# Sums of squares in a decoder trunk: VectorE joins pairs of squared channels into sums of four, TensorE adds two of them in place of four

## The reference, cut to what matters

```python
def rmsnorm(x, g):
    xf = x.astype(jnp.float32)
    y = xf * lax.rsqrt(jnp.mean(xf * xf, axis=-1, keepdims=True) + EPS)
    return (y * g.astype(jnp.float32)).astype(x.dtype)
...
        x = x + rmsnorm(mix, p['norm_mix_post'][l])
        h = rmsnorm(x, p['norm_ffn_pre'][l])
        f, buf = conv_ffn(h, conv_s0[l], p['ffn_w_gate'][l], p['ffn_w_up'][l], p['ffn_conv_w'][l],
                          p['ffn_conv_b'][l], p['ffn_w_down'][l])
        conv_bufs.append(buf)
        x = x + rmsnorm(f, p['norm_ffn_post'][l])
```

## Time and profile before

| what | us |
|---|---|
| median of 3 runs | 1463.52 |
| lowest and highest run | 1462.89, 1463.57 |
| span of the profiled execution | 1460.7 |
| the profiled execution's own time | not given apart from its span |
| TensorE busy | 1424.8 |
| VectorE busy | 910.8 |
| ScalarE busy | 676.9 |
| GpSimd busy | 562.9 |

### The profile page before, as it was taken

How to read it: one execution, slowest core, us unless ns; L and a number is a source line. 1 busy time by engine, 2 the same in 40 slices (tenths; PEclk the granted TensorE clock), 3 DMA queues, 4 the chain that set the end, 5 groups by cost and what they waited for, 6 DMA issues and landing times.

```text
span 1460.7 us, 31008 instructions
## 1 busy us (share of the span) xinstructions
PE 1424.8 (98%) x11156; PEld 1300.5 (89%) x11156; DVE 910.8 (62%) x1506; ACT 676.9 (46%) x1281; POOL 562.9 (39%) x552
## 2 busy tenths in 40 slices
PE   7999999999999999999999999999999999999997
PEld 6999999999999999998986666766989999999997
DVE  5732437599999992226457643443579999995323
ACT  5333345366666672216313544543275666665111
POOL 2342111145555553431330044441325655553433
PEclk9999999999999999999999999999999999999998
DMA  4243322222222333222321099981313222222231
GB/s 167 74 144 99 119 73 102 92 87 88 95 106 89 112 109 100 79 94 83 113 73 33 15 285 289 282 262 40 116 34 116 88 95 106 89 95 99 80 102 64
DMA packets 56714, 160.19 MB, mean 110 GB/s; under 512 B 7633, under 2 KB 27602, under 8 KB 55330
## 3 DMA queue, kind: packets, MB, share of 16 engines
q1 hardware_dynamic: 50466, 137.82, 28.3%
q0 software_dynamic: 6144, 20.98, 4.7%
HBM read 150.72 MB, written 8.05 MB: 109 GB/s over the span
## 4 chain that ended last, share of the span: by engine, by line
PE 45%; DVE 5%; issue 2%; ACT 1%; POOL 0%; SPq 0%; DMA 0%; POOLq 0%; ACTq 0%; DVEq 0%
PE lin L2287 15%; PE lin L2641 12%; PE lin L2859 4%; PE px L2898 2%; PE px L2936 2%; PE lin L2357 1%; PE px L2903 1%; PE px L2867 1%; PE px L2847 1%; PE lin L2813 1%; PE lin L2793 1%; PE px L2414 1%; PE px L2922 0%; PE lin L2830 0%; PE lin L2829 0%
## 5 line engine op out<-in xcount | busy, mean ns | idle before, releaser
L717 POOL TENSOR_TENSOR w_l<-w_raw,w_h 128x1408 fp32r<-128x1408 f32 (+1 forms) x50 | 143.9, 2878 | 271.6 <-ACT w_h L838 150.1
L712 POOL TENSOR_TENSOR w_l<-w_raw,w_h 128x1024 fp32r<-128x1024 f32 (+2 forms) x42 | 108.2, 2575 | 276.7 <-ACT w_h L838 266.9
L2287 PE MATMUL lin<-xg_h,w_h 128*128 128x272 f32 x848 | 194.1, 301 | 13.2 <-DVE xg_l L1458 10.6
L2287 PE MATMUL lin<-xg_l,w_h 128*128 128x272 f32 x848 | 183.5, 288 | 0.0
L2287 PE MATMUL lin<-xg_h,w_l 128*128 128x272 f32 x848 | 183.4, 288 | 0.0
L2641 PE MATMUL lin<-xq_h,w_h 128*128 128x272 f32 x576 | 166.4, 289 | 3.8 <-DVE xq_l L1844 2.2
L2641 PE MATMUL lin<-xq_h,wq_r 128*128 128x272 f32 x864 | 169.3, 289 | 0.6 <-ACT part L1133 0.6
L2641 PE MATMUL lin<-xq_h,w_l 128*128 128x272 f32 x576 | 166.0, 288 | 0.0
L2641 PE MATMUL lin<-xq_l,w_h 128*128 128x272 f32 x576 | 165.4, 287 | 0.0
L2287 PEld LDWEIGHTS lin<-xg_h,w_h 128*128 128x128 f32 x848 | 136.9, 189 | 20.8 <-issue 13.8
L838 ACT ACTIVATE w_h<-w_raw 128x1024 fp32r<-128x1024 f32 (+2 forms) x71 | 77.3, 1089 | 167.1 <-PE lin L2287 140.0
(11 more groups left out here) (407 smaller groups left out, 3231.4 us busy)
## 6 DMA issues: line engine op xcount, KB each, us to landing
wq_raw<-w SPq DMA_DIRECT2D x38, 1024.0 KB, 4.9
w_raw<-w SPq DMA_DIRECT2D x61, 512.0 KB, 3.5
w_raw<-w SPq DMA_DIRECT2D x30, 704.0 KB, 4.1
pages<-cache SPq DMA_DIRECT2D x128, 160.0 KB, 3.8
pages<-cache POOLq DMA_DIRECT2D x128, 160.0 KB, 3.9
St<-state SPq DMA_DIRECT2D x4, 1024.0 KB, 5.6
gla_s<-St SPq DMA_DIRECT2D x4, 1024.0 KB, 3.9
w_raw<-w SPq DMA_DIRECT2D x4, 576.0 KB, 3.6
```

Of the source, the lines that this page charges most:

```text
L712: g.tensor_tensor(w_l[:, p % 2, 0:n], raw_panel(p)[:, 0:n], w_h[:, p % 2, 0:n].bitcast(F32), ALU.subtract).then_inc(w_lo, 1)
L717: g.tensor_tensor(w_l[:, p % 2, 0:n], w_raw[:, p % 2, 0:n], w_h[:, p % 2, 0:n].bitcast(F32), ALU.subtract).then_inc(w_lo, 1)
L2287: last = mm(lin[:, 2 * out_set + half, 0:HALF], w[:, slot, (w0 + k) * P:(w0 + k + 1) * P], (v[ch] if isinstance(v, list) else v[:, ch, :]) ...
```

## The change

The second pair sum of each two is followed by one more addition on VectorE, which joins the two pair sums in `pair_sum[1]` (the tile `rstd_x`) and counts a new semaphore, `quad_sum`. TensorE sums `pair_sum[1]` twice per statistic, after channel 4 and ahead of channel 7, in place of four pair sums. `sums_before` counts two in place of four for the three statistics, and ScalarE's `rstd` waits for two. VectorE's wait on `stat_ps` asks for nothing beyond the earlier statistics at the first three pairs, and for the first of the two sums at the fourth (`m // 3`).

```diff
--- before.py
+++ after.py
@@ -305,6 +305,7 @@
         gla_in = sem("gla_in")
         xh_done, xl_done = sem("xh_done"), sem("xl_done")
         sq_done, sq_used = sem("sq_done"), sem("sq_used")
+        quad_sum = sem("quad_sum")
         stat_ps, stat_ln, rstd_done = sem("stat_ps"), sem("stat_ln"), sem("rstd_done")
         t_done, x_done, xv_done = sem("t_done"), sem("x_done"), sem("xv_done")
         y_out = sem("y_out")
@@ -488,7 +489,7 @@
 
         def sums_before(n):
 
-            return sum(4 if k in BY_PAIR else 1 for k in range(n))
+            return sum(2 if k in BY_PAIR else 1 for k in range(n))
 
         def first_halves(n):
 
@@ -865,7 +866,7 @@
             def rstd(n, width, out, too=None):
 
                 if n in BY_PAIR:
-                    act.wait_ge(stat_ps, sums_before(n) + 4)
+                    act.wait_ge(stat_ps, sums_before(n) + 2)
                 else:
                     act.wait_ge(sq_used, SQ_BASE[n] + SQ_LEN[n])
                 fn(out[:], px[:, 0:2, 0:HALF], ACT.Ln, scale=1.0 / width, bias=col("eps")).then_inc(stat_ln, 1)
@@ -1720,8 +1721,11 @@
                     if ch % 2:
                         i, m = i0 + ch, ch // 2
                         dve.wait_ge(sq_done, i + 1)
-                        dve.wait_ge(stat_ps, sums_before(n + 1) + max(m - 1, 0))
+                        dve.wait_ge(stat_ps, sums_before(n + 1) + m // 3)
                         v.tensor_tensor(pair_sum[m % 2], sq[:, (i - 1) % 2, :], sq[:, i % 2, :], ALU.add).then_inc(sq_used, 2)
+                        if m % 2:
+                            dve.wait_ge(sq_used, i + 1)
+                            v.tensor_tensor(pair_sum[1], pair_sum[0], pair_sum[1], ALU.add).then_inc(quad_sum, 1)
 
             def ffn(layer, pa, ta, pb, tb_, n_stat):
                 f0, us0, ps_, ts_ = layer * FC, layer * US_ALL, pa + 2 * PLAIN, ta + 2 * PLAIN
@@ -2376,15 +2380,14 @@
                 for k in range(DC):
                     pe.wait_ge(xh_done, before + k + 1)
                     if k == DC - 1:
-                        pair_squares(n + 1, k - 2)
-                        pair_squares(n + 1, k)
+                        quad_squares(n + 1, 1)
                     for m in range(DIRECT - 1 if n == 3 and k == DC - 2 else DIRECT):
                         for j in range(k - 1, k + 1) if n == 3 and m and k == DC - 1 else (k,):
                             last = direct_chunk(t + m, w[:, m, :], x_, j, (1,) if j < AHEAD[n] else (0, 1))
                         if k == DC - 1:
                             last.then_inc(tile_done, 1)
-                    if k in (2, 4):
-                        pair_squares(n + 1, k - 1)
+                    if k == 4:
+                        quad_squares(n + 1, 0)
 
             def first_panels(p, t, arrive, n):
 
@@ -2414,12 +2417,12 @@
                     last = mm(px[:, half, 0:HALF], ones[:], src[:, half * HALF:(half + 1) * HALF], start=start, stop=stop)
                 return last
 
-            def pair_squares(n, k):
-
-                if k == 1:
+            def quad_squares(n, k):
+
+                if k == 0:
                     pe.wait_ge(stat_ln, n)
-                pe.wait_ge(sq_used, SQ_BASE[n] + k + 1)
-                ones_matmuls(pair_sum[k // 2 % 2], k == 1, k == SQ_LEN[n] - 1).then_inc(stat_ps, 1)
+                pe.wait_ge(quad_sum, 2 * BY_PAIR.index(n) + k + 1)
+                ones_matmuls(pair_sum[1], k == 0, k == 1).then_inc(stat_ps, 1)
 
             def stat_sum(n):
```

## The result

The changed kernel takes 1477.62 us (median of 4 runs, 1476.68 to 1478.05) against 1463.2 for the kernel before (4 runs, 1462.26 to 1463.57): +14.4 us, ratio 1.010, 95% interval 1.0087 to 1.0114. It lies 2.0 us above the top of the range. The forecast way was right, the size was not. The spans differ by 15.7 (1476.4 against 1460.7), 1.3 more than the medians. The slowest of the four runs, 1478.05, is the profiled one, and 1.65 us lie outside its span. That and the 0.4 by which 1478.05 lies above its own median make the 1.3.

The account below looks back on a forecast made before the run. The prediction took a VectorE and ScalarE chain from pair 2's sum to bound each site's end, not TensorE. Lateness of 3.59 + 1.53 + 3.59 = +8.7 us on 1463.52 gave 1472.2 us, range 1467.6 to 1475.6.

Parts of the forecast that it names:

- What bounds the sites: Events 0, 1, 2 (sites A, B, C): a VectorE and ScalarE chain sets the end; TensorE's removed work is worth 0.
- The tie at A: Event 0, 284 to 304 us: TensorE starts its fourth pair sum at 300.69, VectorE's fourth pair sum ends at 300.63.
- the wait at B: Event 1, 668 to 688 us: TensorE's fourth pair sum starts at 684.02 after idling for VectorE's, begun at 683.25.
- the chain from pair 2: At each site's end: pair 2's sum, squares of channels 6 and 7, pair 3's sum; lateness passes one for one.
- removed sums: Two of four TensorE sums go per site, 0.96 us each, 1.92 together; forecast worth 0.
- First join, +0.77: VectorE's join of pairs 0 and 1, ahead of channel 6's residual: all later VectorE work comes 0.77 us later.
- what it pushes into: Events 0 and 2: channel 7's addition meets GpSimd's w_l, which goes first; pair 2's sum ends at 300.78 at event 0.
- Second join, on the path whole: VectorE's join of pairs 2 and 3, ahead of TensorE's last sum: wholly on the path, 303.50 to 304.22 at event 0.
- The chain's sum, +8.7: Lateness of TensorE's last sum at events 0, 1 and 2: 3.59 + 1.53 + 3.59 = +8.7 us.
- TensorE's clock, not in the sum: 4.5 us idle gaps at events 0 and 2: nothing to about 1.45 us each; nothing taken, 2.9 for both as upper end.
- Rival 3: TensorE's clock falls in one or both long gaps, events 0 and 2: +10.2 to +11.6, 1473.7 to 1475.1 us; chance 18%.
- Nothing taken up behind the sites: Stages behind the sites give nothing back, since VectorE leaves as late as TensorE; the stages between keep their length.

Follow-up runs that it names:

- the second join alone: Changed kernel with only the join of pairs 2 and 3; TensorE sums pairs 0 and 1 apart: 1465.4 us, +2.6 against the kernel before.
- Holding GpSimd alone: Changed kernel, GpSimd's w_l at events 0 and 2 waiting until pair 2 is summed: 1471.01 us, +8.2; with filler matmuls too, 1467.13 us, +4.4.
- fillers: Changed kernel plus useless matmuls ahead of channel 7's wait, nine at events 0 and 2, six at event 1: 1470.99 us, +8.2 against the kernel before.
- the first join alone: Changed kernel with only the join of pairs 0 and 1; TensorE sums pairs 2 and 3 apart: 1470.51 us, +7.8 against the kernel before.
- the kernel with three buffers: Changed kernel with pair 2 in a third buffer and the first join moved behind pair 2: 1472.84 us, +10.1 against the kernel before.

## Why the prediction was wrong, point by point

*What bounds the sites*: right. The tie at A, the wait at B and the chain from pair 2 held in the traces, and removed sums were worth nothing (the second join alone: the last sum 0.83 to 0.85 late at each site, with one sum fewer ahead of it).

*First join, +0.77, and what it pushes into*: right. The addition of channel 7 took 2.89 with GpSimd first. Holding GpSimd alone took 3.8 us away at full clock.

*Second join, on the path whole*: right, 0.83 where 0.76 was written.

*The chain's sum, +8.7*: right to 0.5 (8.2 with fillers; 8.9 by the starts of the last sums). The prediction puts 2.8 us of the time outside the span; that was the median of the runs less the span of a quicker execution, and 1.7 is right. The forecast of the difference doesn't hang on it.

*TensorE's clock, not in the sum*: **this step failed**, in three places. I took nothing, "the shorter gap being the nearer"; the clock fell. The upper end, 1.45 a site "(half of 12.1 less 9.23)", was the term mis-sized: the half rate lasted 6.9 us at A and C, over which 2.6 each were lost, since it began before TensorE's wait had ended (0.50 from 304.00 on, the sum only at 304.45) and then held for some 5.9 us of work; the start of the kernel was no measure of its length. And B was left out. TensorE in the kernel before is done with channel 6's matmuls there at 679.69 + 2.68 = 682.37:

```profile
679.69 2.68 PE L2357 MATMUL lin<-xf_a,kv_raw 128*128 128x272 f32 x11
```

With pair 2's sum gone and the next one forecast for 685.55 that made a gap of 3.2 us. It was 3.08, and B lost 1.5. In all 6.6 us by the trace and 6.2 by the fillers, where the range had room for 2.9. Rival 3 was the mechanism that came true, on top of the forecast's, with the wrong price and 18%.

*Nothing taken up behind the sites*: right; the stretch from A's exit to B's start changed by 0.14 (6.32 late to 6.18 late), from B's exit to C's start by 0.31 the other way.

Open: which gaps make the clock fall. Length alone doesn't say: 2.12 or 2.13, 2.50 and 2.72 us stand in the traces with and without a fall (2.50 without one at B of the second join alone), and 1.83 with one in one of two places. By their times and mean granted clocks, executions of one kernel seem to differ in it too, and the median of such a kernel then depends on how many of its executions had a fall.

## What to carry to other kernels

Before an operation is added to an engine that looks idle two fifths of the time, lay the timelines of all engines over each other at that place: here VectorE's idle 2 us belonged to a GpSimd operation, and an operation of 0.72 us put ahead of them cost 2.0 more by that (3.65 at A against 1.61 at B). Give every wait that a change adds to TensorE a second price, the slow stretch behind it, at every site where a gap of some 2 us or more can arise. Putting two sums together saves TensorE nothing where the last one waits for its input.

## What the runs showed of the hardware

A VectorE operation with two inputs in SBUF and GpSimd's `w_l` exclude each other to the end of the one that came first: 0.72 became 2.88 to 2.90 behind a `w_l`, in five kernels and for two different operations, and `w_l` became 2.85 to 2.87 behind a pair sum. The Trainium skill, SBUF — State Buffer, section "Who interferes with whom", states that a VectorE instruction with two SBUF inputs and a GpSimd instruction that reads SBUF contend, and that the order of issue decides which one is blocked. These traces agree. I had not expected how easily GpSimd gets in between two VectorE operations that follow each other within 0.1 us (297.78, behind 297.15 in the kernel with three buffers).

TensorE's clock can fall behind a wait of 2.1 us, and the same wait 786 us earlier in one execution left it alone (the first join alone, A and C). It stayed at 1.2 GHz for about 3.4 or 6.9 us in the traces. 24 filler matmuls were enough to prevent the fall at all three sites and were faster than none. The Trainium skill, TensorE: Matmul & The Clock Gate, section "The HAM clock gate (the "warmup" mystery)", states that an idle TensorE falls to 1.2 GHz and that work brings 2.4 GHz back. The traces agree: 0.50 begins in a wait or behind one, and 1.00 returns while TensorE works.
